# Down projection of a feed-forward block by seven block products, their weight and operand sums made in earlier stages and kept in DRAM

## The chip, the cores and the metric

The kernel runs on one core of one Trainium2 chip. TensorE (PE) multiplies, VectorE (DVE), ScalarE (ACT) and GpSimd (POOL) do the elementwise work, and SP and ACT issue the DMAs. The metric is the device time of one execution in microseconds, the median of several runs.

## The reference

One layer of two blocks on 1024 tokens of 1024 features, all in float32. The first block joins a gated convolution and sliding-window attention, the second is full attention with a forget gate, a feed-forward part with a convolution, and a gated embedding at its end. The change touches the feed-forward part, whose inner width is 2816:

```python
FFN_DIM = 2816
...
def conv_ffn(x, w_up, conv_w, conv_b, w_down):
    u, g = jnp.split(x @ w_up, [FFN_DIM], axis=-1)
    g = causal_dwconv(g, conv_w, conv_b)
    return (jax.nn.gelu(g, approximate=False) * u) @ w_down
```

## The kernel before

Activations lie feature-major: a tile is 128 features by 1024 tokens, and a token half is 512 columns. Each float32 operand of a product is split into a high and a low part of 128x512, rounded on one engine and subtracted on another, and each step over 128 features is three matmuls (high by high, low weight or low operand by high). So PE work is counted in matmuls of 128x512.

All engines follow orders written out by hand; semaphores join them. The stages that matter here:

- **The convolution's output product** (called the mix stage below), units 8 to 15 of the weight list. A weight unit is 512 KB, loaded by SP into `raw[0]` and `raw[1]` (one half of 256 KB each, free again when the low part of the half before is made) and split by POOL (`split`, L544 and L546). PE fills `bank[0]` and then `bank[1]` (`tile`, L638), DVE empties each (`mixed`, L2474), ACT stores the product and loads the next gate. Five units for window attention follow, then its pair loop.
- **The up loop.** The 22 inner tiles are made as value and gate products. Tiles 0 to 3 are made one by one; from tile 4 on, each *pair* (value and gate of one tile) is done by seven block products instead of eight (`pair`, L957), 84 matmuls. ACT copies the first result out (`first_copy`, L1525), DVE adds the others (`total`, L2333), does the convolution (`tap`, L2601 and L2605), ACT the gelu (L1852), DVE multiplies value and gate (`gated`, L2612), and ACT stores the tile in `h_scr`. `first_copy` of a pair waits for `gated` of the pair before, as both use `up_u`, and PE's fifth block product waits for `first_copy`. POOL makes the sums and low parts of the weights (L549, L559), ACT the high parts (L1520). During the first pair ACT scales the residual `z` (`residual`, L1847).
- **The down stage.** It computes 8 output tiles by 2 token halves from 22 inner tiles: 16 x 22 x 3 = 1056 matmuls (`down_half`, L1122). For each token half PE walks through all weights, 22 units, which POOL splits alone. The 22 operand tiles of a half are loaded from `h_scr` by ACT into small rooms, rounded by ACT (`gated_hi`, L1959) and subtracted by DVE (`gated_lo`, L2695). The first product needs all 22 operands within its 66 matmuls; nearly all of the first half's are made during the last pair and the start of the stage.
- **The gate stage** (`gate_half`, L1148) normalises and multiplies by the embedding's gate; it ends the kernel.

## Time and profile before

| | us |
|---|---|
| median of 3 runs | 2637.88 |
| lowest and highest run | 2637.32, 2639.16 |
| profiled execution, its own time | 2635.02 |
| span of its trace | 2633.2 |

The profiled execution lies 2.9 us under the median, and 1.8 us of its time lie outside the span. All rows are of that one execution, with times counted from the start of the span. PE is the busiest engine by far. A matmul lasts 0.39 us in the rows but overlaps its neighbours, so the pace is read from how far starts lie apart, or from a group's time divided by its count in the chain of waits.

### The profile page before, as it was taken

To read this page: it belongs to the slowest core of one execution; us is meant where nothing else is said; L and a number is where in the kernel's file an instruction comes from. 1 tells how busy PE (TensorE), PEld (TensorE's weight loads), DVE (VectorE), ACT (ScalarE), POOL (GpSimd) and SP (SyncE) were. 2 spreads that over 40 slices of the span, in tenths; PEclk is the share of its full clock that TensorE was granted. 3 is DMA by queue.
4 is the path that set the end of the run, shared out by engine and by line. 5 is a ranking of instruction groups with operands and counts; after the bars stand their busy time and mean duration, and the time that the engine had idled before them with its cause. 6 is when DMAs were issued, how large, how long until landed. Compare 5 with 4: busy or idle time off the path is not lost.

```text
span 2633.2 us, 37256 instructions
## 1 busy us (share of the span) xinstructions
PE 2554.6 (97%) x12046; PEld 2078.2 (79%) x12046; DVE 1402.4 (53%) x2080; ACT 1064.2 (40%) x1940; POOL 1277.9 (49%) x1064
## 2 busy tenths in 40 slices
PE   8999999999999999999999999899999999899998
PEld 5788888887888878888878888777878888687777
DVE  6455542211676675335555555646766565714445
ACT  4333233204666651127777776613333323402121
POOL 3788887333211224431111111144398878577766
PEclk9999999999999999999999999999999999999999
DMA  3221223531000014421111111421222222533333
GB/s 110 80 80 64 66 70 108 192 136 48 30 28 24 32 52 148 144 97 37 37 40 40 40 40 41 148 77 49 68 81 79 84 84 76 191 105 128 123 129 120
DMA packets 101055, 218.72 MB, mean 83 GB/s; under 512 B 11088, under 2 KB 11216, under 8 KB 100960
## 3 DMA queue, kind: packets, MB, share of 16 engines
q1 hardware_dynamic: 72704, 134.77, 16.2%
q10 hardware_dynamic: 28256, 82.75, 8.8%
q8 instruction: 51, 0.84, 0.1%
q14 instruction: 44, 0.36, 0.0%
HBM read 176.52 MB, written 40.96 MB: 83 GB/s over the span
## 4 chain that ended last, share of the span: by engine, by line
PE 84%; DVE 4%; ACT 4%; issue 3%; DMA 2%; POOL 2%; ACTq 0%; DVEq 0%; POOLq 0%; SPq 0%
PE bank L638 20%; PE bank L957 16%; PE bank L701 14%; PE flip L957 8%; PE pv L957 4%; PE pv L1122 3%; PE bank L1148 3%; PE flip L1122 3%; PE pv L902 2%; DMA raw<-in_w 2%; PE score L638 2%; POOL wlo L546 1%; PE score L874 1%; PE flip L887 1%; PE pv L783 1%
## 5 line engine op out<-in xcount | busy, mean ns | idle before, releaser
L544 POOL TENSOR_SCALAR whi<-raw 128x512 fp32r<-128x512 f32 x314 | 233.0, 742 | 1188.1 <-PE bank L701 645.5
L546 POOL TENSOR_TENSOR wlo<-raw,whi 128x512 fp32r<-128x512 f32 x314 | 442.3, 1409 | 26.2
L638 PE MATMUL bank<-a_hi,whi 128*128 128x512 f32 x464 | 185.6, 400 | 3.8 <-POOL wlo L546 2.0
L638 PE MATMUL bank<-b_lo,whi 128*128 128x512 f32 x464 | 183.5, 395 | 0.0
L559 POOL TENSOR_TENSOR wlo<-a,whi 128x512 fp32r<-128x512 f32 x114 | 165.5, 1452 | 13.4 <-ACT whi L1520 12.7
L701 PE MATMUL bank<-b_hi,whi 128*128 128x512 f32 x384 | 155.0, 404 | 5.6 <-DVE fk_lo_odd L2214 3.2
L701 PE MATMUL bank<-b_hi,wlo 128*128 128x512 f32 x384 | 151.6, 395 | 0.0
L701 PE MATMUL bank<-b_lo,whi 128*128 128x512 f32 x384 | 151.3, 394 | 0.0
L638 PE MATMUL bank<-b_hi,whi 128*128 128x512 f32 x336 | 133.3, 397 | 0.4 <-DVE b_lo L2061 0.4
L638 PE MATMUL bank<-a_lo,whi 128*128 128x512 f32 x336 | 133.4, 397 | 0.0
L638 PE MATMUL bank<-a_hi,wlo 128*128 128x512 f32 x336 | 133.1, 396 | 0.0
L1520 ACT ACTIVATE whi<-a 128x512 fp32r<-128x512 f32 x114 | 71.0, 628 | 140.8 <-PE bank L957 60.2
L1400 ACT ACTIVATE fp<-fp,neg_max 128x128 f32<-128x128 f32 (+7 forms) x128 | 99.1, 775 | 26.0 <-DVE neg_max L2256 25.4
L1406 ACT ACTIVATE fp<-fp,row_inv 128x128 f32<-128x128 f32 (+7 forms) x128 | 99.3, 776 | 25.5 <-DVE row_inv L2261 24.8
L638 PEld LDWEIGHTS bank<-a_hi,whi 128*128 128x128 f32 x464 | 87.7, 189 | 27.1 <-issue 3.7
L2252 DVE CUSTOM_DVE_ANT_0 fp<-score,fc 128x128 f32<-128x128 f32 (+7 forms) x128 | 96.6, 755 | 15.3 <-issue 5.4
L638 PEld LDWEIGHTS bank<-b_lo,whi 128*128 128x128 f32 x464 | 87.4, 188 | 20.4 <-POOL wlo L546 0.5
L701 PE MATMUL bank<-a_hi,whi 128*128 128x512 f32 x240 | 98.0, 408 | 3.8 <-DVE s_z L2140 3.8
L701 PE MATMUL bank<-a_hi,wlo 128*128 128x512 f32 x240 | 94.8, 395 | 0.0
L638 PE MATMUL bank<-b_hi,wlo 128*128 128x512 f32 x240 | 94.6, 394 | 0.0
L701 PE MATMUL bank<-a_lo,whi 128*128 128x512 f32 x240 | 94.6, 394 | 0.0
L701 PEld LDWEIGHTS bank<-b_hi,whi 128*128 128x128 f32 x384 | 72.6, 189 | 20.0 <-issue 3.2
(541 smaller groups left out, 7411.0 us busy)
## 6 DMA issues: line engine op xcount, KB each, us to landing
raw<-in_w SPq DMA_DIRECT2D x314, 256.0 KB, 2.6
a<-in_pairs SPq DMA_DIRECT2D x152, 256.0 KB, 2.6
h_scr<-up_y ACTq DMA_DIRECT2D x22, 512.0 KB, 2.6
fc<-c_scr ACTq DMA_DIRECT2D x16, 512.0 KB, 3.6
stage<-h_scr ACTq DMA_DIRECT2D x22, 256.0 KB, 3.6
a<-h_scr ACTq DMA_DIRECT2D x21, 256.0 KB, 3.3
y_scr<-up_y ACTq DMA_DIRECT2D x8, 512.0 KB, 2.6
t_scr<-y_room ACTq DMA_DIRECT2D x8, 512.0 KB, 2.9
```

The costliest lines, as they stand in the source:

```text
L544: nc.gpsimd.tensor_scalar(hi, src, 1.0, 1.0, ALU.mult, ALU.mult).then_inc(w_hi, 1)
L546: nc.gpsimd.tensor_tensor(lo, src, hi.bitcast(F32), ALU.subtract).then_inc(w_lo, 1)
L559: nc.gpsimd.tensor_tensor(ring[1][pos], src[:].rearrange("p (k c) -> p k c", c=P), ring[0][pos].bitcast(F32), ALU.subtract).then_inc(ww_lo, 1)
L638: last = nc.tensor.matmul(psum_ap, ws[w][:, k, :], a[:, kt, hs(h)], start=(first and i == 0 and j == 0), stop=(final and i == n - 1 and j ...
L701: last = nc.tensor.matmul(bank[b][:], ws[slot][:, k, :], a[:, k, hs(h)], start=(k == 0 and j == 0), stop=(k == KT - 1 and j == 2))
L957: last = nc.tensor.matmul(dst[:], ring[w][pos][:, k, :], a, start=(k == 0 and j == 0), stop=(k == KH - 1 and j == 2))
L1122: last = nc.tensor.matmul(down_bank[m % 2][:], w[ws][:, wk, :], a, start=(k == 0 and j == 0), stop=(k == FT - 1 and j == 2))
L1148: last = nc.tensor.matmul(bank[c][:], w[(U_GATE + i) % 2][:, k, :], a, start=(k == 0 and n == 0), stop=(k == KT - 1 and n == 2))
L1400: nc.scalar.activation(fp[s % 3][:, 0:w], fp[s % 3][:, 0:w], ACT.Exp, bias=neg_max[:, one], accum_out=row_sum[:, one]).then_inc(fx.exp, 1)
L1406: nc.scalar.activation(fp[s % 3][:, 0:w], fp[s % 3][:, 0:w], ACT.Copy, scale=row_inv[:, s % 4:s % 4 + 1]).then_inc(fx.prob, 1)
L1520: nc.scalar.activation(ring[0][pos], src[:].rearrange("p (k c) -> p k c", c=P), ACT.Copy).then_inc(ww_hi, 1)
L2252: v.tensor_tensor_reduce(out=fp[s % 3][:, 0:w], in0=score[s % 2][:, 0:w], in1=fc[hh][:, 0:w], scale=SCALE, scalar=-3.0e38, op0=ALU.subtrac ...
```

## The change

The down product is cut in two along output tiles, inner tiles and tokens, and done by seven block products of 4 output tiles by 11 inner tiles (`down_product`), with weights and operands that are blocks or sums of two blocks: 7 x 4 x 11 x 3 = 924 matmuls. Each result is added to one or two blocks of `z` (`RESULTS`, `down_add`).

- **Weight sums.** The four blocks of each of the 11 inner steps are loaded by SP, summed by DVE (`down_sums`, five sums of 128x512) and stored by SP in `wd_scr`, beside the mix stage and the five units behind it. That is 44 loads and 55 stores of 256 KB on SP's queue, between the loads of the weight units. ACT waits for the last of them before its first window exponential.
- **Operand sums.** Inner tiles are paired (4 with 5, 6 with 7, and so on), and tiles alternate between two buffers, `up_y` and `up_odd`. For 8 of the 11 pairs DVE makes five sums of 128x512 in the up loop (`made_top`, `made_row`, `made_diff`, `made_col`, `made_side`), and ACT stores them in `xs_scr`. For the other three pairs the down stage loads both parts and POOL adds them (`operand_sum`).
- **Room for these buffers** is that of the first four residual tiles: ACT writes them to `x_scr` in one DMA of 2 MB in the first pair, DVE waits for it (`row_stored`) ahead of the next `gated`, and SP loads them back in one DMA in the down stage, once the last tile is in `h_scr`. Weight halves 6 and later of the down stage are issued behind it.
- **The down stage's splitting.** Weights come in 77 halves of 256 KB, each 4 inner steps or 12 matmuls. ACT rounds them (`down_high`, once PE has begun half w - 3), POOL subtracts (`down_low`), and the raw halves have four rooms instead of two, from half 4 on.
- The layer norm of token half 0 moves in between block products 5 and 6.

```diff
+KD = FT // 2
+NMP = KT // 2
...
+LO = (*range(FD, FT - 2, 2), 0, 2, FT - 2)
+HI = tuple(f + 1 for f in LO)
+NXS = (FT - FD) // 2 - 1
...
+RESULTS = (((1, 0, 1), (1, 1, -1)), ((0, 1, 1), (0, 0, -1)), ((0, 0, 1), (1, 1, 1)), ((0, 0, 1), (1, 0, 1)), ((0, 0, 1),),
+           ((0, 1, 1), (1, 1, 1)), ((1, 1, 1),))
+NQ = len(RESULTS)
+NPD = NQ * NMP
+NHALF = NPD * KD // 4
+NT = NQ * KD
...
+            def down_blocks(i):
+                for x, room in enumerate(wd_blocks[i % 2]):
+                    if i >= 2:
+                        sp.wait_ge(moved[2 + i % 2], 16 + 48 * (i // 2))
+                    sp.dma_start(room[:], down_weights[x, i, :, :]).then_inc(moved[i % 2], 16)
+            def down_sums_store(i):
+                a11, a12, a21, a22 = wd_blocks[i % 2]
+                for f, (room, kept) in enumerate(((wd_sums[0], 4), (wd_sums[1], 4), (a12, 2 + i % 2), (a22, 2 + i % 2), (a21, 2 + i % 2))):
+                    sp.wait_ge(row_made, KT + 5 * i + f + 1)
+                    sp.dma_start(wd_scr[(0, 2, 3, 1, 4)[f], i, :, :], room[:]).then_inc(moved[kept], 16)
+            for u in range(U_MIX + 1, U_MIX + 5):
+                unit(u)
+            sp.wait_ge(conv_lo, KT)
+            for i in range(2):
+                down_blocks(i)
+            for i in range(KD):
+                unit(U_MIX + 5 + i)
+                if 2 <= i + 1 < KD:
+                    down_blocks(i + 1)
+                down_sums_store(i)
...
+            def down_half(w):
+                room = RAW_OF[w]
...
+                q, i = divmod(w, KD)
+                src = down_weights[BLOCK_OF[q], i, :, :] if FORM_OF[q] is None else wd_scr[FORM_OF[q], i, :, :]
+                sp.dma_start(down_raw[room], src).then_inc(down_in[room], 16)
...
+            for w in range(6):
+                down_half(w)
+            sp.wait_ge(h_stored, 16 * FT)
+            sp.wait_ge(ga_stored, 16 * KT + 16 * 5 * NXS)
+            sp.dma_start(z[:, 0:NMP, :], x_scr[0:NMP, :, :].rearrange("k p c -> p k c")).then_inc(x_whole, 16)
+            for w in range(6, NHALF):
+                down_half(w)
...
+            def down_low(w):
+                pool.wait_ge(w_hi, W_DOWN + w + 1)
+                slot, half = (w // 2 + 1) % 2, slice(w % 2 * 4, w % 2 * 4 + 4)
+                src = down_raw[RAW_OF[w]].rearrange("p (k c) -> p k c", c=P)
+                nc.gpsimd.tensor_tensor(wlo[slot][:, half, :], src, whi[slot][:, half, :].bitcast(F32), ALU.subtract).then_inc(w_lo, 1)
...
+            for w in range(NHALF):
+                down_low(w)
+                q, i = divmod(w, KD)
+                ahead = 3 if q == NQ - 2 else 0
+                if 1 <= q < NQ - 1 and NXS <= i + ahead < KD:
+                    operand_sum((q + 1) * KD + i + ahead)
...
-            def down_half(h, n):
-                v = h * FT + n // 2
-                pe.wait_ge(w_lo, (U_DOWN + v) * 2 + (n % 2 + 1))
...
+            def down_product(n):
+                q, p = divmod(n, NMP)
+                for k in range(KD):
+                    at = n * KD + k
+                    w = at // 4
+                    if n == 4 * NMP + NMP and k == KD // 2:
+                        mean(n2, 0)
+                    if n == 6 * NMP and k == KD // 2:
+                        square_sum(n2, 0, KT - 1)
+                    if at % 4 == 0:
+                        pe.wait_ge(w_lo, W_DOWN + w + 1)
+                    if k == 0 and n >= 2:
+                        pe.wait_ge(down_out, ADDS_UP_TO[n - 2])
                     elif k == 0:
+                        pe.wait_ge(sums_out, 7 * NPR - (0 if n else 4))
+                    if p == 0:
+                        pe.wait_ge(gt_lo, q * KD + k + 1)
+                    ws, wk, slot = (w // 2 + 1) % 2, w % 2 * 4 + at % 4, q % 2 * KD + k
+                    for j, (x, a) in enumerate(((whi, slot_hi[slot]), (whi, slot_lo[slot]), (wlo, slot_hi[slot]))):
+                        last = nc.tensor.matmul(down_bank[n % 2][:], x[ws][:, wk, :], a,
+                                                start=(k == 0 and j == 0), stop=(k == KD - 1 and j == 2))
+                        if at and at % 4 == 0 and j == 0:
                             last.then_inc(down_used, 1)
+                last.then_inc(down_done, 1)
...
+            residual(range(NMP))
+            act.wait_ge(z_alpha, NMP)
+            act.dma_start(x_scr[0:NMP, :, :].rearrange("k p c -> p k c"), z[:, 0:NMP, :]).then_inc(row_stored, 16)
...
+            up_pair(NC + 1, 1)
+            made_store(MADE_SIDE, 0, 1)
+            up_pair(NC + 2, 0)
+            made_even(0)
+            with act.Fori(NC // 2 + 1, NPR // 2 - 1) as it:
+                up_pair(it * 2 + 1, 1)
+                made_odd(it - (NC // 2 + 1))
+                made_store(MADE_SIDE, it - NC // 2, 1)
+                up_pair(it * 2 + 2, 0)
+                made_even(it - NC // 2)
+            residual(range(NMP, KT))
...
+            def operand_hi(t, ahead):
+                q, k = divmod(t, KD)
+                room = ROOM_OF[t]
...
+                if q < 2:
+                    act.wait_ge(product_done, 7 * (NPR - 1) + FREED_BY[t])
+                else:
+                    act.wait_ge(down_done, NMP * (q - 1))
+                nc.scalar.activation(slot_hi[q % 2 * KD + k], stage[room][:], ACT.Copy).then_inc(gt_hi, 1)
+                if ahead and t + ahead < NT:
+                    operand_in(t + ahead)
+            def down_high(w):
+                act.wait_ge(down_in[RAW_OF[w]], DOWN_IN[RAW_OF[w]] + 16 * RAW_OF[:w + 1].count(RAW_OF[w]))
+                if w < 4:
+                    act.wait_ge(product_done, 7 * NPR - 6 + w)
+                else:
+                    act.wait_ge(down_used, w - 3)
+                slot, half = (w // 2 + 1) % 2, slice(w % 2 * 4, w % 2 * 4 + 4)
+                nc.scalar.activation(whi[slot][:, half, :], down_raw[RAW_OF[w]].rearrange("p (k c) -> p k c", c=P),
+                                     ACT.Copy).then_inc(w_hi, 1)
...
+            for t in range(5):
+                operand_hi(t, 4 if t else 0)
+            made_odd(NXS - 1)
+            down_high(0)
+            for w in range(1, 4):
+                for t in (3 + 2 * w, 4 + 2 * w):
+                    operand_hi(t, 4)
+                down_high(w)
+            gelu(FT - 1, up_odd)
+            operand_hi(KD, 4)
+            operand_hi(KD + 1, 4)
+            store(FT - 1, up_odd)
...
+            def down_sums(i):
+                a11, a12, a21, a22 = wd_blocks[i % 2]
+                made = KT + 5 * i
+                dve.wait_ge(moved[i % 2], 16 + 64 * (i // 2 + 1))
+                dve.wait_ge(moved[4], 16 + 32 * i)
+                v.tensor_tensor(wd_sums[0][:], a11[:], a22[:], ALU.add).then_inc(row_made, 1)
+                v.tensor_tensor(wd_sums[1][:], a11[:], a12[:], ALU.add).then_inc(row_made, 1)
+                dve.wait_ge(row_made, made + 2)
+                v.tensor_tensor(a12[:], a12[:], a22[:], ALU.subtract).then_inc(row_made, 1)
+                dve.wait_ge(row_made, made + 3)
+                v.tensor_tensor(a22[:], a21[:], a22[:], ALU.add).then_inc(row_made, 1)
+                dve.wait_ge(row_made, made + 4)
+                v.tensor_tensor(a21[:], a21[:], a11[:], ALU.subtract).then_inc(row_made, 1)
...
+            down_sums(0)
+            for j in range(2, KT):
+                mixed(j // 2, j % 2)
+                down_sums(j - 1)
+            down_sums(KT - 1)
+            down_sums(KT)
...
+            def made_of(x, i, n, a, b, op):
+                dve.wait_ge(ga_stored, i * 80 + 16 * (KT + (4 if n > 4 else 1)) if n > 1 else 16 * KT)
+                v.tensor_tensor(made_rooms[x][:], a, b, op).then_inc(t_made, 1)
...
+            def even_pair(n, i):
+                dve.wait_ge(sums_out, n * 7)
+                gated(n + (TILE_OF - 1), up_u_halves, up_odd)
                 value_sums(n, up_u)
+                dve.wait_ge(up_prod, n * 2 + 2 * TILE_OF)
+                made_top(i)
                 dve.wait_ge(up_conv, n * 3 + 3 * TILE_OF)
+                gate_sums(n, up_u, up_gate, lambda: made_row(i), lambda: made_diff(i))
+                dve.wait_ge(t_made, i * 5 + (8 * KH + 4))
+                taps(n, up_y)
...
+            dve.wait_ge(row_stored, 48 * KT + 16)
+            odd_pair(NC + 1, None)
+            with dve.Fori(NC // 2 + 1, NPR // 2 - 1) as it:
+                even_pair(it * 2, it - (NC // 2 + 1))
+                odd_pair(it * 2 + 1, it - (NC // 2 + 1))
+            even_pair(NPR - 2, NXS - 1)
...
+            def down_add(n):
+                q, p = divmod(n, NMP)
+                dve.wait_ge(down_done, n + 1)
+                if n:
+                    dve.wait_ge(down_out, ADDS_UP_TO[n - 1])
+                for i, h, sign in RESULTS[q]:
+                    m = p + NMP * i
+                    v.tensor_tensor(z[:, m, hs(h)], z[:, m, hs(h)], down_bank[n % 2][:],
+                                    ALU.add if sign > 0 else ALU.subtract).then_inc(down_out, 1)
...
+            for n in range(NMP):
+                down_add(n)
+                operand_lo(range(KD + 2 + 3 * n, min(KD + 5 + 3 * n, 2 * KD)))
+            dve.wait_ge(x_whole, 16 * KT + 16)
+            for q in range(1, NQ - 2):
+                for p in range(NMP):
+                    operand_lo(range((q + 1) * KD + 3 * p, (q + 1) * KD + min(3 * p + 3, KD)))
+                    down_add(q * NMP + p)```

The orders of DVE in the mix stage: `y_room` rows are `mixed`, `wd` rows are the blocks and sums of the down weights. Before, in the loop over tiles:

```order
L2482 ISA
L2471 ISA
L2473 ISA
L2474 TENSOR_TENSOR y_room_156<-bank,xb 128x512 x2
L2471 REGISTER_ALU
L2473 REGISTER_ALU
L2474 TENSOR_TENSOR y_room_157<-bank,xz 128x512 x2
```

And now, one tile with its sums:

```order
L2656 TENSOR_TENSOR y_room_172<-bank,xb 128x512 x2
L2664 TENSOR_TENSOR wd_155<-wd_151,wd_154 128x512
L2665 TENSOR_TENSOR wd_156<-wd_151,wd_152 128x512
L2667 TENSOR_TENSOR wd_152<-wd_152,wd_154 128x512
L2669 TENSOR_TENSOR wd_154<-wd_153,wd_154 128x512
L2671 TENSOR_TENSOR wd_153<-wd_153,wd_151 128x512
L2656 TENSOR_TENSOR y_room_173<-bank,xz 128x512 x2
```

Five sums stand between two tiles' evictions.

ACT at the end of the up loop's first pair: `b_hi` rows are rounded weights, `z` the residual, `up_y` the gelu. Before:

```order
L1520 ACTIVATE b_hi<-a_1_140 128x512
L1520 ACTIVATE b_hi<-raw_50 128x512
L1847 ACTIVATE z<-z,shift 128x1024 x4
L1927 UNCONDITIONAL_BRANCH
L1927 ISA
L1852 ACTIVATE up_y<-up_y 128x1024
```

And now:

```order
L1624 ACTIVATE b_hi<-a_1_140 128x512
L1624 ACTIVATE b_hi<-raw_50 128x512
L1954 ACTIVATE z<-z,shift 128x1024 x4
L2036 DMA x_scr<-z 128x4x1024
L1959 ACTIVATE up_y<-up_y 128x1024
L1624 ACTIVATE whi_52<-a_134 128x512
```

The 2 MB store goes out ahead of the gelu; the multiplication behind that gelu, on DVE, waits for it to land.

ACT where the down stage begins: `t1hi` to `t4hi` are rounded operands, `a` their rooms, `whi` rounded weights. Before, from the last gelu on:

```order
L1852 ACTIVATE up_y<-up_y 128x1024
L1959 ACTIVATE t1hi<-a_136 128x512
L1959 ACTIVATE t1hi<-a_134 128x512
L1959 ACTIVATE t1hi<-a_1_140 128x512
L1959 ACTIVATE t1hi<-a_0_137 128x512
L1959 ACTIVATE t4hi<-up_y 128x512
L1857 DMA h_scr<-up_y 128x1024
```

And now, from weight half 3 on:

```order
L2110 ACTIVATE whi_51<-raw_50 128x512
L1959 ACTIVATE up_odd<-up_odd 128x1024
L2098 ACTIVATE t2hi<-a_133 128x512
L2077 DMA a_0_137<-h_scr 128x512
L2098 ACTIVATE t2hi<-a_136 128x512
L2077 DMA a_133<-h_scr 128x512
L1964 DMA h_scr<-up_odd 128x1024
L2110 ACTIVATE whi_52<-raw_49 128x512
```

ACT now rounds weights too, and half 4 (the last row) stands behind the last gelu and the store of the last tile. On SP's queue the loads at the same place, all of the down weights but one, are now:

```order
L573 DMA raw_49<-wd_scr 128x512
L573 DMA raw_50<-wd_scr 128x512
L582 DMA z<-x_scr 128x4x1024
L573 DMA b_hi_f<-wd_scr 128x512
L573 DMA b_lo_f<-wd_scr 128x512
```

The rows are halves 4 and 5, the reload of 2 MB, and halves 6 and 7 behind it; there was no such reload.

## Rows read from the trace of the kernel before

**Rows 1.** The page, busy time of each engine, and shares of the chain of waits:

```profile
PE 2554.6 (97%) x12046; PEld 2078.2 (79%) x12046; DVE 1402.4 (53%) x2080; ACT 1064.2 (40%) x1940; POOL 1277.9 (49%) x1064
...
PE 84%; DVE 4%; ACT 4%; issue 3%; DMA 2%; POOL 2%; ACTq 0%; DVEq 0%; POOLq 0%; SPq 0%
```

**Rows 2.** Chain of waits in order of time, down stage: start, us, what:

```profile
2291.88 15.33 PE flip L1122 x66
...
2391.09 4.34 DMA raw<-in_w
```

**Rows 3.** Lines L1122 and L1148: duration ns, first to last start; its idle time:

```profile
L1122 PEld LDWEIGHTS pv<-b_hi,whi x100: 186/188/193, 2267.6 to 2507.3; 128*128 128x128 f32 x100
...
  POOL wlo L546: 5.8, 6
...
L1148 PEld LDWEIGHTS bank<-t3hi,whi x32: 186/188/332, 2525.8 to 2579.4; 128*128 128x128 f32 x32
```

**Rows 4.** Timeline of PE, last pair and start of the down stage [idle before]:

```profile
2262.29 0.49 PE L957 MATMUL bank<-t4hi,b_hi 128*128 128x512 f32 x1 [1.49 <-DVE up_u L2333]
...
2286.49 0.77 PE L1122 MATMUL pv<-t1hi,whi 128*128 128x512 f32 x1 [2.72 <-DVE t1lo L2695]
```

**Rows 5.** Stretches: length, busy PE, PEld, DVE, ACT, POOL, granted clock, DMA, GB/s:

```profile
2286.50:2290.00 3.50, 3.50 (x8) 2.49 (x9) 3.50 (x4) 0.00 (x0) 2.00 (x2) 0.51 0.76 226
...
2529.00:2536.00 7.00, 7.00 (x30) 5.34 (x29) 3.36 (x6) 1.83 (x3) 2.31 (x3) 1.00 0.95 325
...
2542.00:2546.00 4.00, 4.00 (x12) 3.08 (x12) 3.60 (x3) 1.88 (x4) 3.50 (x4) 0.57 0.36 131
```

**Rows 6.** Start of the down stage: timeline of ACT, and L2695's durations:

```profile
2263.56 0.63 ACT L1959 ACTIVATE b_hi<-a 128x512 fp32r<-128x512 f32 x1 [1.51 <-DVE b_lo L2695]
...
2281.88 1.06 ACT L1852 ACTIVATE up_y<-up_y 128x1024 f32<-128x1024 f32 x1
...
2284.79 0.36 ACTq L1857 DMA_DIRECT2D h_scr<-up_y  x1
...
L2695 DVE TENSOR_TENSOR b_lo<-a,b_hi x9: 680/693/1778, 2257.2 to 2270.1; 128x512 fp32r<-128x512 f32 x9
```

**Rows 7.** DMA issues, KB each, us to landing; the reload of `x_scr` before:

```profile
h_scr<-up_y ACTq DMA_DIRECT2D x22, 512.0 KB, 2.6
...
L489 SPq DMA_DIRECT2D b_hi_f<-x_scr x8: 339/432/598, 1662.0 to 1665.9; - x8
...
DMA to landing us min/median/max: 4.5/7.3/10.2
```

**Rows 8.** Timeline, first and second pair of the up loop; the last is the chain's:

```profile
1938.45 4.26 ACT L1847 ACTIVATE z<-z,shift 128x1024 f32<-128x1024 f32 x4
...
1943.69 3.44 DVE L2612 TENSOR_TENSOR up_y<-up_y,up_u 128x512 f32<-128x512 f32 x2 [2.48 <-ACT up_y L1852]
...
1947.84 0.60 ACT L1525 ACTIVATE up_u<-bank 128x512 f32<-128x512 f32 x1 [3.15 <-DVE up_y L2612]
...
1948.57 5.73 PE bank L957 x24
```

**Rows 9.** Mix stage: the stretch as in rows 5, timeline of DVE and POOL:

```profile
485.00:597.00 112.00, 112.00 (x483) 90.88 (x482) 24.57 (x29) 10.85 (x13) 35.91 (x36) 1.00 0.43 149
...
541.21 0.69 DVE L2474 TENSOR_TENSOR y_room<-bank,xb 128x512 f32<-128x512 f32 x1 [4.89 <-PE bank L638]
...
542.17 1.29 POOL L546 TENSOR_TENSOR wlo<-raw,whi 128x512 fp32r<-128x512 f32 x1
```

**Rows 10.** Up loop in its steady part: the stretch as in rows 5, timeline:

```profile
1957.00:2247.00 290.00, 290.00 (x1263) 237.23 (x1261) 174.21 (x181) 89.48 (x135) 237.67 (x167) 1.00 0.25 80
...
2238.79 0.69 DVE L2333 TENSOR_TENSOR up_g<-up_u,pv 128x512 f32<-128x512 f32 x1 [1.28 <-PE pv L957]
...
2231.16 1.06 ACT L1852 ACTIVATE up_y<-up_y 128x1024 f32<-128x1024 f32 x1 [2.84 <-DVE up_y L2605]
```

**Rows 11.** Line L2612, additions of SBUF operands beside POOL's: min, median, max ns:

```profile
L2612 DVE TENSOR_TENSOR up_y<-up_y,up_u x42: 678/1753/1840, 1867.5 to 2283.6; 128x512 f32<-128x512 f32 x42
```

433 lines of the change are left out of this document (253 added, 180 removed).

## The prediction

> **What bounds the kernel now.** I read the busy shares and the chain of waits first: PE is busy for 97% of the span and makes up 84% of the chain [rows 1]. So what counts is how many matmuls PE has, at what pace, and where it is left waiting. The pace is in the chain's pieces of the down stage: 66 matmuls take 15.33 us, 0.2323 each [rows 2]. The stage runs from 2267.6 to the first load of the gate stage at 2525.8, 258.2 us [rows 3]; its 1056 matmuls at that pace are 245.3, so 12.9 are losses. Of these, 7.0 are at the start: the matmul at 2286.49 is the 52nd and would have begun at 2279.5 (51 x 0.2323 after 2267.6); it waited for low parts of operands from DVE [rows 4]. Some 1.7 us follow because the clock is down: over the next 3.5 us the granted clock is 0.51, the lower of the two levels [rows 5]. The rest is weights that come late: the chain has pieces of 4.34 us in which POOL waits for a raw load [rows 2], and PE's idle time behind POOL's low parts is 5.8 us in six waits [rows 3].
>
> **1. Fewer matmuls.** 1056 - 924 = 132 fewer, x 0.2323 = **-30.7 us**, all on the path. Nothing in shape or operands differs, so the pace should hold.
>
> **2. The down stage in its steady part.** A weight half lasts PE 12 x 0.2323 = 2.79 us. In that time ACT has one half (0.63 us) and one operand (0.63) to round [rows 6] and one or two loads to issue, POOL one low part (1.29) [rows 9], DVE 2.75 low parts of 0.69 [rows 6] per product of 7.67 us and one to three adds of about 0.7. All fit. Weights are rounded three halves (8.4 us) ahead of PE, loads four. So I expect no waits from about half 8 on, where there are several now. What stays are the two ends of the norm's small matmuls and the handover to the gate stage, whose first weights can be split only when PE starts its last half: two halves on POOL, 4 x about 1 us, against 2.79. I take 3.0 for all of this (now about 4.2 of the 12.9).
>
> **3. The down stage's start.** It is worse than now, by two chains.
> - *Weight half 4* stands on ACT behind the last gelu and the store of the last tile. Before, that gelu began at 2281.88 and the store was issued at 2284.79 [rows 6]. DVE now has 11 low parts and one sum ahead of it instead of 17, five operations fewer at about 0.9 (0.69 alone, up to 1.78 beside POOL [rows 6]), so the store goes out near 2280.3. Half 4 is rounded by 2281.3 and its low part made near 2282.8. PE, beginning at 2267.0, wants it after four halves, at 2278.2: a wait of 4.6, with what DVE still delays before it inside that.
> - *Weight half 6* is issued behind the reload of 2 MB, which waits for the last tile to land: 2280.3 + 2.6 [rows 7] = 2282.9. Such traffic ran at 325 GB/s with the engines 95% busy [rows 5], so 2.1 MB are 6.5 us, the half 0.8, and about 1.0 of fixed time (a 512 KB store lands after 2.6, of which 1.6 are bytes). That is 2291.2 if SP has the engines alone, and up to 6.5 later if ACT's operand loads take half. The reload of `x_scr` before, 4.2 MB in eight DMAs issued from 1662.0 to 1665.9 and landed by 10.2 later [rows 7], 14.1 us in all, is of the same rate. I take 2293.5, and 2296.0 after rounding and low part. PE wants it at 2267.0 + 16.7 + 4.6 = 2288.3: a wait of 7.7.
> - After such a wait the clock is at its lower level for 3.5 to 4 us [rows 5], about 1.7 lost.
>
> Start: 4.6 + 7.7 + 1.7 = 14.0; with part 2, 17.0 instead of 12.9: **+4.1 us**. Bounds: 8 (the reload is quick) and 20 (ACT's loads take their half) for the 14.0. The Trainium skill ("DMA: Bandwidth & Descriptors", section "Queues, rings and completion order") says that SP and ACT have one ring each on the same 16 DMA engines, and that each engine takes its ring in order and goes round between rings. By that half 6 cannot pass the reload, and ACT's loads take up to a half; no row here shows the two together. If a free engine served half 6 at once, this part would be 7.7 + 1.7 smaller.
>
> **4. The last pair.** DVE has three low parts instead of four ahead of the sums that PE waited 1.49 us for [rows 4]. **-0.9 us**.
>
> **5. The store of the residual, first pair of the up loop.** The order rows show it ahead of the gelu. Now: residual until 1942.7, `gated` on DVE from 1943.69, `first_copy` at 1947.84, and PE goes on at 1948.57 [rows 8], when it could have at about 1948.1. So from `gated`'s start to PE are 4.9 us, and PE has no slack there. The store is issued at 1943.0 and lands 6.5 + 1.0 later, plus 0.9 for the weight loads beside it: 1951.4. `gated` begins 7.7 later. I take 6.7, as its two adds (1.7 us each beside POOL, 0.68 alone [rows 8, 11]) may meet POOL less, and 1.7 for the clock: **+8.4 us**. Bounds 5 and 11. Nothing hides this: PE's next product needs the bank that `first_copy` empties.
>
> **6. The mix stage.** Five sums per tile on DVE, which is busy for 24.6 us of 112 [rows 9]. Alone they take 5 x 0.69 = 3.5 us, beside POOL's split (which starts at the same moment [rows 9]) perhaps 6. DVE idles 4.89 before an eviction [rows 9], and the eviction may be another 5.6 late before PE, on the other bank, wants the first one back. So the arithmetic costs nothing. The transfers are the question. Per tile: four loads and five stores of 256 KB, a weight unit of 512, the product's store and a gate's load of 512 each, 3.93 MB. At 325 GB/s that is 12.1 us, while PE has 48 matmuls or 11.15 us. Over seven tiles the queue falls 6.6 us behind. A weight unit has slack: POOL's split takes some 4 us of 11, and SP loads a unit ahead; sums are used a tile later than their blocks land. I put the slack at 5 us, and the cost at **+1.5 us**; bounds 0 and 8. In the units for window attention there is less traffic and DVE idles; ACT's wait for the last sum is about 4 us ahead of need. Nothing there.
>
> **7. The up loop.** Five sums per two pairs. DVE has gaps of 1.28 to 2 us between the sums of a pair, where they are placed, and ACT 2.84 ahead of the gelu, for 2 or 3 issues of about 0.45 [rows 10]. Each room's store has about 5 us to land before DVE wants the room again. **0 us**; bounds 0 and 4. POOL is busy for 237.7 of 290 us [rows 10], so it idles 3.5 per pair; DVE's additions beside it last up to 1.8 us instead of 0.68 [rows 11], and each new one may hold it up likewise, 2.5 x 1.1 = 2.8 per pair. That is close, and a rival below. The Trainium skill ("SBUF — State Buffer", section "SBUF: two separate sides") has the mechanism: a DVE operation with two SBUF inputs and a GpSimd one exclude each other for a whole instruction. By it the hold-up is at most the new sums' own 0.7 each, 1.7 per pair, and the rival falls away; [rows 11] agree in that the long ones are about a GpSimd operation longer.
>
> **The sum.** -30.7 + 4.1 - 0.9 + 8.4 + 1.5 = -17.6. From the profiled execution's 2635.0 that gives 2617.4; it lies 2.9 below the median, so in medians 2637.9 - 17.6 = **2620**.
>
> **Rivals.**
> - *A. Both long waits are cheap*: the store lands before it hurts (5 instead of 8.4) and halves 6 and 7 come in time (8 instead of 14), no loss in the mix stage. 2620 - 3.4 - 6 - 1.5 = 2609, or a bit below if the start gains on DVE's shorter list. For: DVE's list is shorter, transfers often beat my additions. Against: both orders are plain.
> - *B. The mix stage is paced by its transfers*: each tile 12.5 to 13 us instead of 11.15, 7 to 14 us in all over its slack: 2632.
> - *C. GpSimd becomes the bound of the up loop*: if each new sum costs it 1.8 instead of 1.1 us, a pair is 4.5 against 3.5 idle, 1 us longer over 17 pairs: 2637, no change.
> - *D. Slower: SP's queue in the mix stage.* SP waits for each of DVE's sums, and behind that stand the next weight unit and the next blocks. If loads and stores together move at 225 GB/s instead of 325, a tile's 3.93 MB take 17.5 us, 6.3 over PE's, less 5 of slack over seven tiles: +39, about 2658. It decides from 276 GB/s down (14.2 us a tile, where the gain is used up). Against it: a stretch at 325 with loads only [rows 5]; for it: none with stores mixed in is in the trace.
>
> That the seven products don't do what they say is no case: the count is fixed by the orders.
>
> **How the numbers follow.** Forecast (2612 to 2629) 0.56, A 0.18, B 0.12, C 0.07, D 0.07. The range takes the forecast, A, and B: 2606 to 2637, about 0.85. A measurement tells about 0.2% (5.3 us) from no change: faster is below 2632.6. Faster 0.56 + 0.18 + 0.10 = 0.86 with a little of C, same 0.07, slower 0.07.
>
> **What would show it.** In the profile after: the down stage from first matmul to the gate stage about 232 us, with 66 matmuls still in 15.33; a PE wait of 4 to 5 us at half 4 and 5 to 9 at half 6, behind ACT's rounding and the raw load; no waits for weights from half 8 on. One wait of 6 to 8 us in the first pair of the up loop, behind `gated` and the store. Mix stage within 2 us of now. It is wrong if PE waits in steady pairs for low weights (C), if evictions of the mix stage come late behind sums that wait for loads (B, D), or if half 6 is there when PE asks.

## The result and the profile after

| | before | after |
|---|---|---|
| median, us (12 runs each) | 2639.09 | 2629.60 |
| lowest and highest run | 2635.24, 2643.15 | 2622.82, 2634.38 |
| profiled execution: time, span | 2635.02, 2633.2 | 2630.32, 2628.5 |

The ratio is 0.9964, 95% interval 0.9955 to 0.9973: 9.5 us faster, where 17.6 were forecast. The time lies in the range; the size is little more than half.

The page after, busy time of each engine, against [rows 1]:

```profile
PE 2531.5 (96%) x11914; PEld 2056.7 (78%) x11914; DVE 1545.4 (59%) x2240; ACT 1125.9 (43%) x2050; POOL 1245.5 (47%) x980
```

PE has its 132 matmuls fewer, and 23.1 us less busy time. The span fell by 4.7 us only, so PE waits longer. The simplest way to see where is to take the start of the first and last matmul of each stage, by line, and to list the gaps between starts; a gap here is the distance between the starts of two neighbouring matmuls, 0.23 us where PE runs at pace. Weight halves are counted from 0, so half 4 is the fifth. A second profile of each kernel (`b0_before`, `e0_after` below) stands beside the first:

| us from start to start | before | b0_before | after | e0_after |
|---|---|---|---|---|
| convolution's products, the mix stage among them | 559.07 | 559.07 | 559.10 | 559.10 |
| from there to the up loop's pairs (not touched) | 1258.53 | 1262.98 | 1262.10 | 1263.07 |
| up loop | 351.42 | 353.74 | 358.00 | 357.60 |
| down stage | 257.88 | 255.26 | 238.76 | 239.63 |
| handover to the gate stage | 0.23 | 0.24 | 2.05 | 2.03 |
| gate stage | 101.56 | 101.71 | 105.85 | 104.72 |

The last four together fell by 6.4 us in the first pair of profiles and by 7.0 in the second. They are split otherwise in the second: before's own last pair of the up loop waits 2.84 us there instead of 1.88, with the lower clock behind that, and its down stage waits less at its start. So the up loop is 3.9 us longer and not 6.6, and the down stage 15.6 shorter and not 19.1.

**First pair of the up loop.** The timeline of DVE and ACT after, against [rows 8]: start, us, instruction, [idle before]:

```profile
1944.92 0.40 ACTq L2036 DMA_DIRECT2D x_scr<-z  x1
...
1952.21 2.37 DVE L2814 TENSOR_TENSOR up_y<-up_y,up_u 128x512 f32<-128x512 f32 x2 [8.82 <-DMA x_scr<-z]
...
1955.07 0.60 ACT L1629 ACTIVATE up_u<-bank 128x512 f32<-128x512 f32 x1 [7.60 <-DVE up_y L2814]
...
1955.79 0.79 PE L1064 MATMUL bank<-t1hi,b_hi 128*128 128x512 f32 x1 [5.50 <-ACT up_u L1629]
```

The gated tile waits for the 2 MB store, the first copy for the tile, PE for the copy: a gap of 5.90 where it was 0.90.

**Start of the down stage.** The chain of waits in order of time:

```profile
2288.46 3.83 DMA h_scr<-up_odd
...
2292.31 0.39 SPq L582
...
2292.74 8.86 DMA b_hi_f<-wd_scr
...
2301.62 0.64 ACT whi L2110
...
2302.33 1.28 POOL wlo L706
...
2303.65 9.18 PE pv L1233 x27
```

and PE at halves 4 and 6:

```profile
2291.04 0.51 PE L1233 MATMUL flip<-b_hi,whi 128*128 128x512 f32 x1 [1.64 <-POOL wlo L706]
...
2303.65 0.79 PE L1233 MATMUL pv<-b_hi,whi 128*128 128x512 f32 x1 [6.76 <-POOL wlo L706]
```

Weight half 6 stands behind the reload (L582), as forecast. PE's gap is 7.16 us; half 4 made one of 2.03. Then 27 matmuls take 9.18 us instead of 6.27 [rows 2]. SP issues half 6 only after its wait for the last tile's store, and the half lands 8.9 us later, 0.7 us after the reload's own landing (8.6 us after its issue at 2292.31). Later in the stage the same loads land 2.8 us after their issue in the median, at most 4.8.

**Sixth block of the down stage**, which the prediction has no wait for; the chain again:

```profile
2451.76 1.29 DVE z L2950 x2
...
2453.51 4.78 DVE z L2217 x8
2458.29 1.22 DVE b_lo L2940 x2
...
2459.53 0.33 ACTq L2077
...
2459.90 4.32 DMA b_hi_f<-h_scr
...
2464.29 1.77 POOL stage L713
2466.06 1.24 POOL wlo L706
...
2467.34 2.93 PE pv L1233 x6
```

and what ACT and PE show at its two ends:

```profile
2459.36 0.63 ACT L2098 ACTIVATE b_hi<-stage 128x512 fp32r<-128x512 f32 x1 [8.24 <-DVE b_lo L2940]
...
2467.34 0.80 PE L1233 MATMUL pv<-t3hi,whi 128*128 128x512 f32 x1 [6.55 <-POOL wlo L706]
```

DVE makes three residues (L2940: low parts of operands) of the last block's gated tiles, waits for the block's first product, does the layer norm's eight centrings (L2217) and only then the fourth residue. ACT stands before a load (L2077) that needs the fourth one's room. The load belongs to a pair that POOL has to add (L713), and the next weight half (L706) stands behind that sum. Four engines in order, and PE starves for 6.95 us.

**Handover.** POOL can split the first gate weight only from 2513.47, when PE starts the last half, and PE's gap is 2.05. ACT issued the gate factors of the first half from 2482.6 on before; after, from 2511.66, since its weight halves stand ahead of them.

```profile
2513.47 0.62 POOL L733 TENSOR_SCALAR whi<-raw 128x512 fp32r<-128x512 f32 x1 [4.43 <-PE flip L1233]
...
2517.45 0.50 PE L1252 MATMUL bank<-t4hi,whi 128*128 128x512 f32 x1 [1.65 <-POOL wlo L735]
...
2535.16 0.79 PE L1252 MATMUL bank<-t4hi,whi 128*128 128x512 f32 x1 [3.66 <-POOL wlo L735]
```

**The clock.** Stretches after the three long gaps, columns as in [rows 5]:

```profile
1956.00:1961.00 5.00, 5.00 (x12) 3.91 (x13) 3.41 (x4) 0.70 (x2) 4.25 (x3) 0.50 0.35 128
...
2303.70:2308.70 5.00, 5.00 (x12) 3.94 (x13) 5.00 (x6) 2.41 (x5) 4.94 (x3) 0.50 0.72 226
2467.40:2472.40 5.00, 5.00 (x12) 3.95 (x13) 1.53 (x2) 3.01 (x4) 5.00 (x4) 0.50 0.38 104
```

The granted clock is 0.50, the lower level, and starts lie 0.427 us apart instead of 0.232 for 12 or 13 matmuls: 2.6 to 2.8 us lost after each gap, not the 1.7 that I had read from before. In `e0_after` the same three gaps are followed by 9 to 11 such matmuls and cost 1.9 to 2.3 us.

**What went as forecast.** The mix stage and the steady up loop, against [rows 9, 10]:

```profile
485.00:597.00 112.00, 112.00 (x483) 90.81 (x482) 51.24 (x59) 9.56 (x11) 41.04 (x38) 1.00 0.81 282
...
1976.00:2262.00 286.00, 286.00 (x1245) 233.86 (x1244) 210.56 (x216) 89.33 (x134) 243.40 (x162) 1.00 0.34 113
```

and the steady down stage, the chain of waits:

```profile
2312.83 7.67 PE flip L1233 x33
...
2427.86 7.67 PE pv L1233 x33
```

From 2312.8 to 2446.7 no piece of that chain is anything but PE at pace. Traffic in the mix stage went from 149 to 282 GB/s, and PE is busy in all of it. A pair of the up loop takes 19.33 us in both kernels.

### The profile page after: what moved, and what is told of

It is laid out like the page before. It is cut to its first block and busy times, and to the rows that moved or that the text cites. A ratio compares the mean times of both kernels' runs of the same rounds, so it can differ in the third digit from the quotient of the medians.

```text
span 2628.5 us, 36803 instructions
## 1 busy us (share of the span) xinstructions
PE 2531.5 (96%) x11914; PEld 2056.7 (78%) x11914; DVE 1545.4 (59%) x2240; ACT 1125.9 (43%) x2050; POOL 1245.5 (47%) x980
## 5 line engine op out<-in xcount | busy, mean ns | idle before, releaser
L625 POOL TENSOR_SCALAR whi<-raw 128x512 fp32r<-128x512 f32 x194 | 148.3, 764 | 1080.9 <-PE bank L808 645.1
L627 POOL TENSOR_TENSOR wlo<-raw,whi 128x512 fp32r<-128x512 f32 x194 | 274.5, 1415 | 16.2
L1624 ACT ACTIVATE whi<-a 128x512 fp32r<-128x512 f32 x114 | 71.1, 628 | 140.2 <-PE bank L1064 60.9
L2444 DVE TENSOR_TENSOR fp_lo<-flip,fp_hi 128x512 fp32r<-128x512 f32 (+1 forms) x96 | 57.5, 599 | 53.6 <-ACT fp_hi L1518 52.8
## 6 DMA issues: line engine op xcount, KB each, us to landing
fc<-c_scr ACTq DMA_DIRECT2D x16, 512.0 KB, 3.6
```

What stands on the lines that cost most here:

```text
L625: nc.gpsimd.tensor_scalar(hi, src, 1.0, 1.0, ALU.mult, ALU.mult).then_inc(w_hi, 1)
L627: nc.gpsimd.tensor_tensor(lo, src, hi.bitcast(F32), ALU.subtract).then_inc(w_lo, 1)
L1624: nc.scalar.activation(ring[0][pos], src[:].rearrange("p (k c) -> p k c", c=P), ACT.Copy).then_inc(ww_hi, 1)
L2444: v.tensor_tensor(fp_lo[:, blk:blk + nb, s % 2, :], flips[n % 2][:, 0:nb * P].rearrange("p (b c) -> p b c", c=P), fp_hi[:, blk:blk + nb, s ...
```

## The experiments

All times are medians, and `...` in code stands for lines that are not shown; before's in the same group of runs is 2639.88 (first four), 2638.58 (next four), 2643.07 (next three) and 2640.14 (last). The changed kernel has 2629.60 and 2629.79, ratios 0.9964 and 0.9963.

**The same two kernels again.**

> The changed kernel once more, as the measure for the edits that run beside it. The two profiles so far differ by 4.7 us in span, but by 9.5 us in the medians. Stage by stage (starts of the first and last matmul of each stage) the profiles give: up loop +6.5, down stage with its handover -17.2, gate stage +4.2, together -6.5, and +3.6 between 657 and 1918 us, where the change touches nothing, -1.4 before 98 us. Theory: the 3.6 and the -1.4 are the execution's own scatter, so this profile shows the stages from 1918 us on again within 0.5 us (first up pair 19.4 us instead of 11.8, down stage 239.2, gate stage 106.2) and its untouched stages elsewhere within 4 us. Rival: the change costs something between 657 and 1918 us, and the 3.6 us come back. Time about 2630, 9 to 10 us under the kernel before.

> The kernel before once more, for a second profile of it. Five profiles of the changed kernel and of single edits to it give 1261.7 to 1265.0 us from the first matmul of the window attention to the last product before the up loop, the one profile of before 1258.5, although the change touches nothing there. Theory: that stretch scatters from execution to execution in either kernel, by 3 us and more in parts without any edit (175.0 to 178.7 us from 1657 us on), and the one profile of before, 4 us under its median, was a short draw: this one gives 1259 to 1265. Rival: the change itself costs 3 us or more there, and this profile gives 1258 to 1259 again. The gate stage should take 101.6 us and its handover 0.2, the down stage 257.9, the first up pair 11.8.

Measured: 2629.79, ratio 0.9963 (0.9951 to 0.9975); the table above. The untouched stretch took 1262.98 in before's second profile: theory held, its first was short. In all profiles of this study it takes 1258.5 to 1265.0, a scatter of more than half of what is to be explained, so single edits below are judged by their stage first. (The first pair's 19.4 and 11.8 us, in the expectations here and below, are not the time of all its 84 matmuls: the pair that holds the gap takes 27.7 us instead of 20.1, and 27.3 in `e0_after`. The difference of 7.6 us is right.)

**DVE's order in the sixth block.**

```diff
-            operand_lo(range(first, first + 3))
+            operand_lo(range(first, first + 6))
             down_add(5 * NMP)
-            for j in range(KT):
+            for j in range(3):
                 centre(n2, 0, j)
-            operand_lo(range(first + 3, first + 8))
+            operand_lo(range(first + 6, first + 8))
+            for j in range(3, KT):
+                centre(n2, 0, j)
```

> VectorE's order in the sixth block of the down stage: the residues of six of the last block's gated tiles are made ahead of the eight layer-norm centrings instead of three, the next two after three centrings. Nothing is left out. Theory: the 6.95 us gap of TensorE at 2460.4 is a chain of four engines: VectorE makes the fourth residue only after the 4.86 us of centrings, ScalarE stands for 8.2 us at the load that needs that residue's room, the loads land 4.3 to 5 us after it, and GpSimd holds the next weight half behind the sum of that pair of loads. Then the gap goes (rest of it below 1 us), and with it the 2.6 us that the 13 matmuls at half clock behind it cost: down stage 239.2 to about 230, time 9 us less than the changed kernel's, about 2620.5. Rival one: the loads themselves are late (two loads and a sum take 7.8 us after ScalarE's copy whatever VectorE does), then a gap of 3 to 4 us stays and the gain is 3 us. Rival two: the gap only moves to a later half, behind the centrings that now come later; then the gain is under 1 us.

Measured: 2623.74, ratio 0.9942 (0.9929 to 0.9956), 6.1 us under `e0_after`. The gap is gone, the down stage takes 231.8 instead of 238.8 and 239.6. One of 1.21 us came new, at a weight half behind ACT's squares:

```profile
2477.41 1.41 POOL wlo L706
...
2478.87 3.75 PE pv L1233 x15
```

The theory holds, with a small part of rival two; rival one fell.

**The first half's gate factors early.**

```diff
+                if w == 70:
+                    act.wait_ge(gt_lo, NT)
+                    act.wait_ge(down_done, NMP * (NQ - 1))
+                if 70 <= w < 74:
+                    for m in range(2 * (w - 70), 2 * (w - 70) + 2):
+                        act.dma_start(ple[0][m], ple_scr[m, :, hs(0)]).then_inc(p_in, 16)
...
-            act.wait_ge(gt_lo, NT)
-            act.wait_ge(down_done, NMP * (NQ - 1))
-            for m in range(KT):
-                act.dma_start(ple[0][m], ple_scr[m, :, hs(0)]).then_inc(p_in, 16)
```

> ScalarE's eight loads of the first half's gate factors (2 MB) are issued two each after weight halves 70 to 73 of the down stage, some 28 us before they are now issued (2511.7 us, after the last weight half). Nothing is left out. Theory: the gate stage is 4.2 us longer than before and its handover costs 1.9 more because these loads run beside the first weight loads of the gate stage (4.2 us from issue to landing instead of about 2.6) and hold ScalarE's squares for 13.3 us. Then the gate stage comes back to about 102 us, the handover keeps its 1.6 us (it is set by GpSimd's splits behind the last weight half), and the time falls by 4 us against the changed kernel, to about 2625.5. Rival: the gate stage's waits are GpSimd's own (its two splits of a half weight take 4.4 us from the time the slot is free), or the second 2 MB of such loads, which now come 10 us earlier, take the place of the first: then less than 1.5 us.

Measured: 2629.52, ratio 0.9961 (0.9947 to 0.9975), no gain in time; gate stage 103.98 (105.85 and 104.72 without the edit), handover 2.06. My theory of the gate stage fell: the second and third product still wait, 1.54 and 3.98 us.

**The reload behind ten halves.**

```diff
-            for w in range(6):
+            for w in range(10):
                 down_half(w)
...
-            for w in range(6, NHALF):
+            for w in range(10, NHALF):
                 down_half(w)
```

> The 2 MB reload of the residual stands behind the first ten weight halves on SyncE's queue instead of six. Nothing is left out. Theory (a term of the prediction, there 7.7 us and 1.7 of clock): half 6 waits because it is queued behind the reload, which itself waits until the last gated tile's store has landed. Then the wait of 6.8 us at 2296.5 goes, and the 2.6 us at half clock behind it: down stage 239.2 to 229.8, time 9.4 us less than the changed kernel's, about 2620. Rival one: the ten halves behind it meet the same wait at half 10 (landed 8.9 us after the reload's issue, with only four halves or 11 us of work in stock): then 1 to 3 us stay. Rival two: half 6 is late by its own room or by bandwidth, and the gain is under 2 us.

Measured: 2621.43, ratio 0.9928 (0.9914 to 0.9943), 8.4 us less; down stage 229.7. The gap at half 6 is gone and 1.67 us stay at the eleventh half, the first behind the reload now:

```profile
2296.20 0.39 SPq L582
...
2296.63 12.17 DMA b_hi_f<-wd_scr
```

That is the forecast's mechanism, and rival one's size of rest. The edit takes half 6 out from behind two things at once, the reload and SP's wait for the last tile's store ahead of it, and doesn't tell their shares.

**The wait for the residual's store, later in the pair.**

```diff
+                if i is None:
+                    dve.wait_ge(row_stored, 48 * KT + 16)
                 following = 0 if i is None else i + 1
...
-            dve.wait_ge(row_stored, 48 * KT + 16)
             odd_pair(NC + 1, None)
```

> VectorE's wait for the 2 MB store of the residual is moved in the first pair of the up loop from ahead of the gated tile's products to ahead of the first sum that writes into the stored rooms, some 9 us later in its order. Nothing is left out. Theory (a term of the prediction, 6.7 us of wait and 1.7 of clock; the profile shows 5.0 and 2.6): VectorE stands for that store, the gated tile, and with it the first copy and TensorE, wait behind it. Then the pair takes 11.8 us again instead of 19.4, and the time falls by 7.6 us, to about 2622. Rival one: ScalarE's first copy is late by itself, because its queue issues the 2 MB store and the weight highs: then 2 to 4 us stay. Rival two: the wait comes back at the sums, and half of it stays.

Measured: 2621.53, ratio 0.9933 (0.9919 to 0.9946); the up loop takes 350.15 us, and 356.8 to 358.1 in all profiles of the changed kernel that keep the wait where it was. The gated tile begins as it should, and the store costs DVE half a microsecond where it now waits:

```profile
1945.52 2.78 DVE L2814 TENSOR_TENSOR up_y<-up_y,up_u 128x512 f32<-128x512 f32 x2 [3.14 <-ACT up_y L1959]
...
1951.43 0.69 DVE L2511 TENSOR_TENSOR up_g<-up_u,pv 128x512 f32<-128x512 f32 x1 [0.54 <-DMA x_scr<-z]
```

**POOL's splits at the handover**, and the same with the first half's factors loaded early (as in `e2_ple`) and the second half's spread.

```diff
-                for b in range(2):
+                for s in range(2):
+                    b = 1 - s if i == 1 else s
-                    if b == 0 and i == 0:
-                        pool.wait_ge(down_used, NHALF - 1)
-                    elif b == 0 and i == 1:
+                    if i == 0:
+                        pool.wait_ge(down_used, NHALF - 2 + s)
+                    elif s == 1 and i == 1:
                         pool.wait_ge(down_done, NPD)
...
```

(and on SP the loads in the same order into `raw[1 - s]`; this is `e6_split`.)

> At the change from the down stage to the gate stage GpSimd splits each half of the first gate weight as soon as its own half of the slot is free (after 75 and 76 weight halves instead of 76 for both), and splits the other half of the second weight ahead of the one that waits for the last product; SyncE loads the second room first, which is free 8 us earlier. Nothing is left out. Theory: TensorE's wait of 2.05 us between the stages, and a part of the waits of 2.5 and 4.1 us at the second and third gate product, are GpSimd's: it can only begin when the last weight half is in use, 2.8 us before the end, and four instructions take 4.4 us. Then the handover falls to about 0.2 us and the gate stage by another 1 to 2: together 3 us less than the changed kernel, about 2626.5. Rival: the loads of the gate factors beside them set these waits (4 to 5 us to landing instead of 2.6), then the handover alone gains, under 2 us, and the third gate product waits as long or longer.

> The edit of e6_split, with the first half's gate factors loaded at halves 70 to 73 (as in e2_ple) and the second half's eight loads spread one by one over the gate products instead of in a row at its start. Nothing is left out. Theory: with GpSimd's order mended the waits that are left at the second and third gate product are the transfers' (raw loads of 256 KB beside 2 MB of factors in a row at about 300 GB/s). Then both go, and the gate stage is shorter than before's 101.6 us, which has a wait of 3.95 us of the same kind: 98 us, handover 0.2, so 8 to 9 us less than the changed kernel, about 2621. Rival: GpSimd's splits, 3.9 to 4.4 us of a product's 5.57, have no slack to catch up from a late start and hold the waits: then no more than 4 us.

Measured: `e6_split` 2625.08, ratio 0.9946 (0.9932 to 0.9959), handover 0.49, gate stage 104.0; `e7_gate` 2625.72, ratio 0.9955 (0.9942 to 0.9969), handover 0.46, gate stage 103.0. The handover was POOL's. The second product's wait is still 2.72 us in `e6_split` and gone in `e7_gate`, so it was the transfers'; the early loads alone had left 1.54 of it, and spreading the second half's alone was not run. The third one's stayed in `e7_gate`, 3.95 us, and the profile puts it down to POOL. But POOL was ready. POOL, ACT and PE in `e7_gate`:

```profile
2523.45 1.29 POOL L737 TENSOR_TENSOR wlo<-raw,whi 128x512 fp32r<-128x512 f32 x1
...
2529.74 0.69 ACT L2178 ACTIVATE b_hi_f<-bank,cst 128x512 f32<-128x512 f32 x1
...
2530.53 0.77 PE L1254 MATMUL bank<-t4hi,whi 128*128 128x512 f32 x1 [3.55 <-POOL wlo L737]
```

PE begins 0.1 us after ACT has copied the first product out of the bank, and in the program that copy stands behind five squares of the norm. Before has the same wait (3.95 us at 2537.8).

**ACT's order in the gate stage.**

```diff
+            gate_out(0)
             for j in range(KT):
                 square_to_sum(n2, 1, j)
-                if j == 4:
-                    gate_out(0)
-            gate_out(1)
+                if j == 3:
+                    gate_out(1)
             gate_store(0)
             gate_out(2)
+            gate_store(1)
+            gate_out(3)
...
```

> In the gate stage ScalarE copies the first gate product's bank out ahead of the eight squares of the layer norm instead of after the fifth, the second after the fourth square, the fourth ahead of the root, the later ones a step earlier between the norm's tiles; each output tile is stored one product later. The same instructions in another order; nothing is left out. In e7_gate the third gate product still waited 3.95 us although GpSimd had its weights ready 5.8 us before: it began 0.1 us after ScalarE's copy of the first product's bank had ended, and that copy stood behind five squares, which stand behind VectorE's eight centrings. Theory: this wait (4.06 us in the changed kernel, 3.95 in the kernel before) and the three of 2.0, 1.6 and 2.7 us behind it are the two banks', held by ScalarE's order, and go: the gate stage falls from 105 us to about 96 to 98, the time by 7 to 9 us, to about 2622. Rival: GpSimd's splits or the transfers of the gate factors take the place of the bank: then 2 us or less.

Measured: 2626.97, ratio 0.9937 (0.9923 to 0.995); gate stage 101.8, 2.9 and 4.1 us less than without the edit. Of the three later gaps, 2.0, 1.6 and 2.7 us, none stays; one of 1.29 came new. The third product still waits, 4.87 us, now for a weight that lands late beside the factors (the gate weights' loads take up to 7.8 us to land there, 2.4 at the least):

```profile
2524.78 1.28 ACT L2174 ACT_TABLE_LOAD   x1 [15.07 <-DMA b_hi_f<-ple_scr]
...
2528.58 0.62 POOL L733 TENSOR_SCALAR whi<-raw 128x512 fp32r<-128x512 f32 x1 [5.35 <-issue]
```

So that wait has two causes of about one length, and taking away either alone leaves it at 3.95 or 4.87 us (without either edit it is 2.9 to 5.0 us from profile to profile); theory and rival are each half right.

**Together.**

> The edits of e1_order, e3_reload, e4_upwait and e7_gate together. Nothing is left out. Alone they gave 6.0, 8.4, 8.1 and about 4 us against the changed kernel (each the difference of the medians, those of the second group set against the first by the kernel before). Theory: the four waits stand at different places and for different reasons, so they add up: about 26 us less than the changed kernel, 2603 to 2606, and the down stage takes 239.2 less 9.4 and 7 us, 223 us, for a floor of 214.6 at pace. Rival: the stages behind are paced by something that has had the time of these waits to run ahead (VectorE's sums and the loads of gated tiles in the down stage), and a third or more of the sum comes back as new waits there.

> The edits of e8_four and e9_evict together, and ScalarE's copy of the down stage's fifth weight half put ahead of the last gelu instead of behind it, two copies and the last store. Nothing is left out. Theory: another 2.0 us at the down stage's start and 6 to 8 in the gate stage: about 2595, 1.6% under the kernel before, with the gate stage at 93 to 96 us for a floor of 89.2 at pace. Rival: half 5 or 6 is late instead of half 4, since their rooms come free only behind the copies that are now moved back: then the first 2 us stay.

> The edits of e10_best without the moved copy of the fifth weight half. Nothing is left out. In e10_best TensorE waited 1.44 us there instead of 2.03, but another 3.16 us at the eleventh half, whose load stands behind the 2 MB reload and landed 13.1 us after it was issued; without the moved copy (e8_four) there was no such wait and the down stage took 222.2 us instead of 225.3. Theory: starting earlier at half 4 only makes TensorE arrive earlier at the half that the reload holds up, and the moved copy costs 3.1 us net: this kernel's down stage takes 222.2 again, its gate stage 94.3, its time is 2593, 3 us less than e10_best. Rival: the 3 us between the two down stages are scatter of that transfer from execution to execution (the eleventh half waited 1.67 us in e3_reload with the same order): then the time is that of e10_best within 1 us and the wait at the eleventh half is back at 1 to 3 us.

| | time | ratio (95%) | up loop | down stage | handover | gate stage |
|---|---|---|---|---|---|---|
| e8_four | 2602.07 | 0.9842 (0.9829 to 0.9856) | 350.12 | 222.19 | 0.42 | 101.74 |
| e10_best | 2595.87 | 0.9820 (0.9806 to 0.9833) | 350.12 | 225.27 | 0.49 | 94.28 |
| e11_last | 2594.60 | 0.9827 (0.9814 to 0.9841) | 350.11 | 222.20 | 0.45 | 94.05 |

The waits add up: the last four stages of `e8_four` take 674.5 us and those of the changed kernel 704.7 and 704.0, and no new long wait comes up behind them. The third gate product no longer waits with both its causes gone. In `e10_best`, with the copy of half 4 moved, the gap of 2.03 at half 4 went and one of 1.44 came at half 5, as its rival has it, and 3.16 at the eleventh half:

```profile
2285.72 0.50 PE L1235 MATMUL flip<-t2hi,whi 128*128 128x512 f32 x1 [1.04 <-POOL wlo L707]
...
2302.69 0.69 PE L1235 MATMUL flip<-b_hi,whi 128*128 128x512 f32 x1 [2.76 <-POOL wlo L707]
```

Without the moved copy the down stage is 222.20, as `e11_last` expected. That the copy costs these 3 us rests on one profile: of three profiles in the other order two have no wait at the eleventh half and `e3_reload` has 1.67. In the times they don't show: the medians are 1.3 us apart, and the ratios' intervals overlap. `e11_last` is 1.7% faster than the kernel before, where the change as made gains 0.36%.

## Why the prediction was right and wrong

Sizes in us, from the first pair of profiles:

| part | forecast | measured |
|---|---|---|
| 1 matmuls | -30.7 | -30.7 (66 matmuls still 15.34) |
| 2, 3 losses of the down stage with handover | +4.1 | +13.4 |
| 4, 5 up loop | +7.5 | +6.6 |
| 6 mix stage | +1.5 | 0.0 |
| 7 steady up loop | 0 | 0 |
| gate stage | not costed | +4.3 |
| sum | -17.6 | -6.4 |

**Right:** the direction, part 1, and both places where the change adds a wait with what makes it. The pair with the store's gap takes 27.7 us instead of 20.1, so part 5 is 7.6, forecast 8.4, split otherwise: 5.0 of wait and 2.6 of clock. Part 4 is -1.1 in the first pair of profiles (the gap fell from 1.88 to 0.81), forecast -0.9. At the down stage's start I had 12.3 of waits and 1.7 of clock, 14.0 in all; it is 13.0: 1.8 + 6.9 of waits, 2.7 of clock after the second, and 1.5 in short waits for halves 1 and 2 and in steps of 0.34 us beside them and half 4. No matmul runs at the lower clock between half 4's gap and half 6's. So the waits were 3.6 us shorter than forecast and the rest 2.5 longer: that the sum came so near is in part luck.

On the ring order: half 6 landed 8.9 us after its issue behind the reload, where such a load lands after 2.8 otherwise. The Trainium skill's "DMA: Bandwidth & Descriptors", section "Queues, rings and completion order", has each ring served in order; the trace agrees.

**Wrong, the step that failed:** "All fit. [...] So I expect no waits from about half 8 on". I had compared each engine's work per half with PE's 2.79 us and found room on all four. That is a statement about busy time, but the engines take their lists in order. In the sixth block DVE's list puts 4.8 us of centrings between two residues, and ACT's and POOL's lists hang on the second. A delay of one list then passes through two others, with a load and a sum on the way, and is longer than the stock of three weight halves, 8.4 us. It cost 6.7 us and 2.8 of clock, 9.5 in all, where the term had nothing (7.6 and 1.9 in `e0_after`). Up to that point the term held: between half 9 and half 60 no gap is longer than 0.64 us in either profile. `e1_order` moves only those instructions of DVE, and its stage is 7.4 us shorter than the mean of the two profiles without the edit.

**Missing:** the gate stage. I costed its handover (in the 3.0; with the stage's other rests it is 3.7) and took the stage behind it as before. The change makes ACT's and POOL's lists run up to the last product, so that what they had done ahead of time before (the factors' loads, the first weights) comes after it. The prediction followed the lists for the store, half 4 and the reload, and not past the stage's end. What of the 4.3 belongs to which cause is not settled further than the experiments show: transfers at the second product, both transfers and ACT's order at the third, ACT's order at three later ones. Of these only the wait at the second product (2.5 and 2.05 us) is new in both profiles. Before has the third (3.95, 4.17) and the later three (0.9, 2.3 and 1.2) too, and in `e0_after`, whose stage is 3.0 us longer than before's, the later three are as long as before's.

**Not located:** the stages give -6.4 and -7.0, the medians -9.5 and -10.1. 1.2 us of the rest are in seven units between 1190 and 1657 us, 466.9 and 467.0 before, 465.7 and 465.6 after, though the change touches nothing there; all ten profiles of the edits have it as short as after, so it isn't the scatter of single executions, and its cause is open. The remaining two are within what the untouched stretch scatters.

**The rivals.** A's two cheap waits didn't come true (7.6 and 13.0 us where it had 5 and 8), its mix stage without loss did. B and D fell with the convolution's products at 559.1 us in both kernels: 282 GB/s in the mix stage and no wait, so the 1.5 us of part 6 were not there. C fell too: POOL's busy time per pair rose from 15.8 to 16.4 us (237.67 in 290 us [rows 10], 243.40 in 286), 0.6 for two and a half sums that I had priced at 2.8. The Trainium skill's "SBUF — State Buffer", section "SBUF: two separate sides", has a VectorE operation with two SBUF inputs and a GpSimd operation that reads SBUF exclude each other for a whole instruction. An estimate from that page, with this case's 0.7 us a sum, is 1.7 us at the most, and the trace agrees.

## What to carry to other kernels

Where every engine works through a fixed list, room in busy time doesn't show that a stage is free of waits: go through the lists at each place where another kind of work (here a norm) is set in between, and ask who waits for the instruction behind it, and who for that one. When work is moved onto an engine up to a stage's end, look at what that engine used to do there for the next stage. Look at the profile's releaser with the program beside it: a wait put down to one engine ended with another's copy, and it had a second cause of the same length, so only the two edits together removed it.

## What the runs showed of the hardware

The transfers are faster than the 325 GB/s that I took as their rate. While the reload and the loads of both queues ran in `e8_four`, columns as in [rows 5]:

```profile
2289.00:2299.00 10.00, 10.00 (x44) 8.08 (x43) 6.18 (x7) 2.31 (x4) 3.59 (x3) 1.00 1.03 407
```

The cost of the lower clock after a wait is not fixed by the wait's length. In the up loop, the down stage and the gate stage of all 14 profiles, gaps of 2.84 to 8.7 us were followed by 6 to 13 matmuls at 0.427 us (1.4 to 2.8 us lost), the long ones by no more than the short ones. Gaps of 1.9 to 2.2 us, half 4's in all eleven profiles that have it among them, were followed by none. Between these it went either way: those of 2.27 or 2.28 us were followed by 7 or 8, most of 2.5 to 2.8 us by none and one of 2.67 by 8.
